# A two-block transformer on one core: latent and cross-attention queries computed turned, the first feed-forward steps reordered, the input loaded in quarters

## The reference

```python
# block 1
h = h + 0.5 * swiglu(rmsnorm(h, ffn1_norm), ffn1_w_gu, ffn1_w_down)   # hidden width 2816
# ... sparse and block attention of 8 heads each, gates, w_out ...
h = h + 0.5 * swiglu(rmsnorm(h, ffn2_norm), ffn2_w_gu, ffn2_w_down)
# block 2, layer 0 mixer: latent attention (8 heads, 128 + 64 rope dimensions)
lat = h @ w_dkv
c_q, c_kv, k_pe = rmsnorm(lat[:384], g_q), rmsnorm(lat[384:640], g_kv), lat[640:]
q, kv = c_q @ w_uq, c_kv @ w_ukv
# causal softmax over [q, rope(q_pe)] . [k, rope(k_pe)], then @ w_o
# layer 1 mixer: stick-breaking attention. After each mixer:
h = h + mem_cross_attn(rmsnorm(h), rmsnorm(mem), w_q, w_kv, w_o)      # 4 heads of 128, 256 memory rows
h = h + square(relu(rmsnorm(h) @ w_in)) @ w_out                       # hidden width 4096
```

## Time and profile before

| | |
|---|---|
| time, median of 3 runs | 1272.52 us (1272.42 to 1272.82) |
| profiled execution: time | 1272.93 us |
| profiled execution: span of its instructions | 1271.0 us |
| PE busy | 1257.9 us (99%) |
| PE weight loads busy | 1081.4 us |
| DVE busy | 756.7 us (60%) |
| ACT busy | 656.1 us (52%) |
| POOL busy | 21.1 us |

### The profile page before, as it was taken

How to read it: one execution, slowest core, us unless ns; L and a number is a source line. 1 busy time by engine, 2 the same in 40 slices (tenths; PEclk the granted TensorE clock), 3 DMA queues, 4 the chain that set the end, 5 groups by cost and what they waited for, 6 DMA issues and landing times.

```text
span 1271.0 us, 16754 instructions
## 1 busy us (share of the span) xinstructions
PE 1257.9 (99%) x6734; PEld 1081.4 (85%) x6734; DVE 756.7 (60%) x1056; ACT 656.1 (52%) x846; POOL 21.1 (2%) x25
## 2 busy tenths in 40 slices
PE   9999999999999999999999999999999999999997
PEld 7888888888888888889888799989888887999896
DVE  6555448788675554447765675454553655754553
ACT  6454437464455444436954564443465745643433
POOL 0000000001000000000000000000000000000001
PEclk9999999999999999999999999999999999999999
DMA  8855546554533655544633265554565332665540
GB/s 291 291 178 197 185 151 209 217 182 138 177 133 125 242 180 195 179 135 169 240 125 116 83 240 192 199 177 135 185 232 184 115 108 91 226 216 176 195 133 34
DMA packets 39213, 221.71 MB, mean 174 GB/s; under 512 B 4486, under 2 KB 5142, under 8 KB 23649
## 3 DMA queue, kind: packets, MB, share of 16 engines
q1 hardware_dynamic: 36672, 214.20, 48.8%
q0 software_dynamic: 1024, 4.22, 1.0%
q10 hardware_dynamic: 1440, 2.22, 0.6%
HBM read 219.56 MB, written 1.07 MB: 174 GB/s over the span
## 4 chain that ended last, share of the span: by engine, by line
PE 93%; DVE 3%; ACT 2%; issue 1%; DMA 1%; POOL 0%; SPq 0%; DVEq 0%; ACTq 0%
PE ps L403 23%; PE ps L405 23%; PE ps L404 23%; PE ps L612 5%; PE ps L611 5%; PE ps L610 5%; PE ps L1424 2%; PE ps L1449 2%; PE ps L437 1%; DVE wlo L368 1%; PE ps L984 1%; PE ps L1436 1%; PE ps L643 1%; DMA w_raw<-ffn_first 1%; ACT whi L360 0%
## 5 line engine op out<-in xcount | busy, mean ns | idle before, releaser
L368 DVE TENSOR_TENSOR wlo<-w_raw,whi 128x2048 fp32r<-128x2048 f32 (+4 forms) x244 | 468.5, 1927 | 379.2 <-ACT whi L360 379.0
L360 ACT ACTIVATE whi<-w_raw 128x2048 fp32r<-128x2048 f32 (+4 forms) x244 | 393.3, 1618 | 407.3 <-PE ps L405 304.9
L403 PE MATMUL ps<-whi,xt_h 128*128 128x512 f32 (+3 forms) x784 | 308.8, 394 | 1.5 <-DVE nat L790 0.8
L405 PE MATMUL ps<-whi,xt_l 128*128 128x512 f32 (+3 forms) x784 | 302.5, 386 | 0.0
L404 PE MATMUL ps<-wlo,xt_h 128*128 128x512 f32 (+3 forms) x784 | 301.8, 385 | 0.0
L403 PE MATMUL ps<-whi,ot_h 128*128 128x512 f32 x594 | 235.1, 396 | 0.0
L405 PE MATMUL ps<-whi,ot_l 128*128 128x512 f32 x594 | 231.7, 390 | 0.0
L404 PE MATMUL ps<-wlo,ot_h 128*128 128x512 f32 x594 | 231.4, 390 | 0.0
L403 PEld LDWEIGHTS ps<-whi,xt_h 128*128 128x128 f32 x784 | 147.3, 188 | 32.7 <-issue 4.8
L405 PEld LDWEIGHTS ps<-whi,xt_l 128*128 128x128 f32 x784 | 147.1, 188 | 29.6
L404 PEld LDWEIGHTS ps<-wlo,xt_h 128*128 128x128 f32 x784 | 147.4, 188 | 27.3
(11 more groups left out here) (227 smaller groups left out, 875.7 us busy)
## 6 DMA issues: line engine op xcount, KB each, us to landing
w_raw<-ffn_mid SPq DMA_DIRECT2D x80, 768.0 KB, 4.3
w_raw<-mlp_mid SPq DMA_DIRECT2D x56, 1024.0 KB, 5.0
w_raw<-w_qkv SPq DMA_DIRECT2D x12, 1024.0 KB, 5.0
w_raw<-w_sb_qkv SPq DMA_DIRECT2D x12, 1024.0 KB, 4.9
w_raw<-w_xkv SPq DMA_DIRECT2D x8, 1024.0 KB, 4.9
w_raw<-ffn_first SPq DMA_DIRECT2D x8, 512.0 KB, 4.4
w_raw<-w_gate_b SPq DMA_DIRECT2D x4, 1024.0 KB, 4.9
w_raw<-w_gate_a SPq DMA_DIRECT2D x4, 1024.0 KB, 5.0
```

Of the source, the lines that this page charges most:

```text
L360: nc.scalar.activation(whi[:, s, 0:tiles * width], w_raw[:, s, 0:tiles * width], ACT.Copy).then_inc(w_hi, 1)
L368: nc.vector.tensor_tensor(wlo[:, s, 0:tiles * width], w_raw[:, s, 0:tiles * width], whi[:, s, 0:tiles * width].bitcast(F32), ALU.subtract) ...
L403: nc.tensor.matmul(acc, hi, whi[:, s, c], start=start, stop=False)
L405: return nc.tensor.matmul(acc, lo, whi[:, s, c], start=False, stop=stop)
```

## The change

It has four parts.

1. **Latent queries and keys turned** (`LatentUp` in place of the `Project` named `mla_up`). The rope queries come first, in the usual form. The eight query heads and the eight key heads are made in the turned form, two heads (a pair) per bank. A token's row factor can no longer be applied per partition. For the queries it moves into the exponent's scale and the peak (`row`, `minus`); for the keys it is spread over partitions by two products (`diagonals` against ones) and multiplied in by DVE when it takes the keys out of the bank (`take_k`).
2. **Cross-attention queries turned**, head by head, row factor in the exponent; the fourth head's products stand between the scores; the groups are ordered by pair of heads; DVE scales all four; the projection's pieces are reordered.
3. **First step of the gated feed-forwards**: in ffn2 the last two chunks go by token tile (`second_half`); in ffn1 the products of a tile run as high parts first (`first_tensor`), and chunk 4's low part is split in two pieces around `nat` of tile 0 (`second_lo`).
4. **x in four quarters**, one between each two of the first weight chunks; chunks 0 to 2 are split tile by tile; three wake products instead of two behind the first transposes.

The core of the diff:

```diff
+            def tensor(self, pe):                                  # LatentUp
+                before = self.before
+                pe.wait_ge(before.lows, NT)
+                for t in range(NT):
+                    pe.wait_ge(before.evac, t + 1)
+                    self.rows(pe, self.pe, t, 0, 3)
+                before.turn(pe, before.units[-1])
+                for p in range(4):
+                    pe.wait_ge(self.evac, p + 1)
+                    self.pair(pe, self.q[p // 2], p, 0, 3)
+                self.aside.tensor(pe)
...
+                pe.wait_ge(self.diagonal, 1)
+                for t in range(NT):
+                    last = nc.tensor.matmul(bankT[0][:, t * P:(t + 1) * P], const[:, C_ONES:C_ONES + P],
+                                            self.diagonals[:, t * P:(t + 1) * P], start=True, stop=True)
+                last.then_inc(self.spread, 1)
+                for p in range(4):
+                    if p < 2:
+                        pe.wait_ge(self.evac, 5 + p)
+                    else:
+                        pe.wait_ge(self.k_taken, p - 1)
+                    self.pair(pe, self.k[p // 2], p, 3, 2)
+                self.turn(pe)
...
+            def scalar(self, act):
...
+                next_hi(act, self.q[1])
+                self.aside.scalar(act)
+                act.wait_ge(self.spread, 1)
+                nc.scalar.activation(self.factors, bankT[0][:, 0:S], ACT.Copy).then_inc(self.spread_in, 1)
+                next_hi(act, self.k[0])
+                self.take_turned(act)
+                act.wait_ge(self.before.rooted, 2)
+                self.take_v(act, 0)
+                next_hi(act, self.k[1])
+                self.take_v(act, 1)
+                next_hi(act, self.v[0])
+                next_hi(act, self.v[1])
...
+            def vector(self, dve):
+                self.factor(dve)
+                self.rotate(dve, 0)
+                self.rotate(dve, 1)
+                next_lo(dve, self.pe)
+                next_lo(dve, self.q[0])
+                next_lo(dve, self.q[1])
+                self.aside.vector(dve)
+                self.take_k(dve, 0)
+                self.take_k(dve, 1)
+                next_lo(dve, self.k[0])
+                self.take_k(dve, 2)
+                self.take_k(dve, 3)
+                next_lo(dve, self.k[1])
+                next_lo(dve, self.v[0])
+                next_lo(dve, self.v[1])
```

```diff
             def tensor(self, pe):                                  # CrossAttention
...
+                self.query(pe, [0, 1], [2, 3])
+                self.query(pe, [2], [0, 1, 2, 3])
+                take_chunk(pe, self.q0 + 1)
+                self.query(pe, [0, 1, 2], [4, 5])
+                self.query(pe, [0, 1, 2], [6, 7])
                 pe.wait_ge(*self.keys_ready)
+                pe.wait_ge(cross_taken, NXH * i + 2)
                 att.score(pe, 0)
                 att.score(pe, 1)
+                used(self.query(pe, [3], [0, 1, 2, 3]), self.q0)
+                self.query(pe, [3], [4, 5, 6, 7])
+                att.turn(pe, 0)
+                pe.wait_ge(cross_taken, NXH * (i + 1))
                 att.score(pe, 2)
                 att.score(pe, 3)
+                att.turn(pe, 1)
                 pe.wait_ge(*self.values_ready)
                 att.value(pe, 0)
+                att.value(pe, 1)
                 att.turn(pe, 2)
                 att.turn(pe, 3)
                 att.value(pe, 2)
                 att.value(pe, 3)
```

```diff
+                if self.name == "ffn1":                            # Ffn.vector, behind the root
+                    second_lo(dve, 0)
+                    self.hide_vector(dve, 0, (0,))
+                    second_lo(dve, 1)
+                    self.hide_vector(dve, 0, (1,))
                 else:
-                    next_lo(dve, self.n0)
-                self.hide_vector(dve, 0)
+                    if self.gated:
+                        next_lo(dve, self.n0)
+                    self.hide_vector(dve, 0)
...
+            for part in range(3):                                  # ACT's start; DVE's is alike
+                pair_scalar(act, "ffn1", part)
+                first_hi(act, part)
+            pair_scalar(act, "ffn1", 3)
             split_hi(act, 3)
...
-            wake(2)
-            norm_tensor(pe, "ffn1", 0, (1,))
+            wake(3)
```

More of the change, by code:

```diff
@@ L294, in build @@
         ident_in = sem("ident_in")
-        x_in = [sem(f"x_in{part}") for part in range(3)]
-        first_tile = sem("first_tile")
+        x_in = [sem(f"x_in{part}") for part in range(4)]
+        tile_hi = sem("tile_hi")
+        tile_lo = sem("tile_lo")
         blanks = sem("blanks")
@@ L2132, in gpsimd @@
                 pass
-        class CrossAttention:
-            def __init__(self, i, fills, q_unit, groups, fins, like=None):
-                self.cross, self.mlp = f"cross{i}", f"mlp{i}"
-                self.q = Project(f"mem_q{i}", f"xq{i}", [q_unit], xt_h, xt_l, norm=self.cross)
-                self.unit = q_unit
-                self.att = Attend(f"mem{i}", groups, fins, [], turned=True, bare=True, like=like and like.att)
-                self.fin, self.keys_ready, self.values_ready = self.att.fin, fills[0].ready, fills[1].ready
-                self.n0 = AT[f"xo{i}"]
-                self.full = sem(f"mem_out{i}_full")
-                ends[self.n0], ends[self.n0 + 1] = (self.full, NT), (self.full, NB * NT)
-            def query(self, pe, n, t, ks):
-                for k in ks:
-                    if t == 0 and k % 2 == 0:
-                        xt_ready(pe, self.cross, k)
-                    last = mm3(bankA[t], xt_h[:, k, t * P:(t + 1) * P], xt_l[:, k, t * P:(t + 1) * P],
-                               slot_of(n), k % 4, TW, k == 0, k == KC - 1)
-                if ks[-1] == KC - 1:
-                    last.then_inc(self.q.full, 1)
+        cross_q = sem("cross_q")
@@ new lines, in build, with __init__, q_bank, query @@
+        cross_taken = sem("cross_taken")
+        cross_out_hi = sem("cross_out_hi")
+        cross_out_lo = sem("cross_out_lo")
+        cross_full = sem("cross_full")
+        class CrossAttention:
+            def __init__(self, i, fills, groups, like=None):
+                self.i, self.cross, self.mlp = i, f"cross{i}", f"mlp{i}"
+                self.att = Attend(f"mem{i}", groups, [], [], turned=True, bare=True, like=like and like.att)
+                self.keys_ready, self.values_ready = fills[0].ready, fills[1].ready
+                self.q0, self.n0 = AT[f"xq{i}"], AT[f"xo{i}"]
+                self.full0 = NB * NT * i
+                ends[self.q0 + 1] = (cross_q, NXH * (i + 1))
+                ends[self.n0], ends[self.n0 + 1] = (cross_full, self.full0 + NT), (cross_full, self.full0 + NB * NT)
+            def q_bank(self, head):
+                return (bankA + bankT)[head][:, 0:S]
+            def query(self, pe, heads, ks):
+                for head in heads:
+                    for k in ks:
+                        if head == 0 and k % 2 == 0:
+                            xt_ready(pe, self.cross, k)
+                        cols = slice(k % 4 * TW + head * P, k % 4 * TW + (head + 1) * P)
+                        n = slot_of(self.q0 + k // 4)
+                        nc.tensor.matmul(self.q_bank(head), whi[:, n, cols], xt_h[:, k], start=k == 0, stop=False)
+                        nc.tensor.matmul(self.q_bank(head), wlo[:, n, cols], xt_h[:, k], start=False, stop=False)
+                        last = nc.tensor.matmul(self.q_bank(head), whi[:, n, cols], xt_l[:, k], start=False,
+                                                stop=k == KC - 1)
+                    if ks[-1] == KC - 1:
+                        last.then_inc(cross_q, 1)
@@ L2587, in mla_groups @@
                         group.append(dict(
-                            at=i * keys, width=keys, tile=t, head=hd,
+                            at=i * keys, width=keys, tile=t, head=hd, row=qrow(t), minus=mla_up.minus(0, t),
                             bias=const[:, C_CAUSAL + S - keys:C_CAUSAL + S],
```

442 lines of the change are left out of this document (291 added, 151 removed).

## The result

| | before | after |
|---|---|---|
| median of 17 runs | 1272.76 us (1272.34 to 1273.16) | 1274.70 us (1274.13 to 1275.87) |
| ratio to before | | 1.0017, 95% interval 1.0011 to 1.0024 |
| profiled span | 1271.0 us | 1272.6 us |

The forecast was 1273.6, 1269.6 to 1276.6, and the result lies inside the 0.2% that the prediction called no change. The sum came close, but two of its terms were too small, in opposite directions.

The account below looks back on a forecast made before the run. It took TensorE's own work (93% of the chain) and its few waits as the bound. Latent +3.4, cross-attentions -2.2, ffn2 0, start -0.2 gave +1.0: 1273.95 profiled, median 1273.6 us, range 1269.6 to 1276.6.

Parts of the forecast that it names:

- likeliest case: The exchange as summed over all stages, without any rival: 55%.
- Latent stage: Latent up-projection to first attention turn: 2.3 us less TensorE work, but waits on DVE; net +3.4, between +2.7 and +4.2.
- first pause: Latent stage, ahead of key pair 2: TensorE waits about 4.0 us for DVE's take_k(0).
- Pairs 2 and 3 (2.9 and 0.1 of restart): Latent stage: key pairs 2 and 3 behind TensorE's wait take 2.9 us plus 0.1 of restart, ending at 626.4.
- The clock rival: The granted clock falls in the latent stage's new pause, costing 2.9 us more: 1276.5; chance 10%.
- The second pause: At the first attention turn TensorE, there at 641.8, waits 2.3 us for a turn at 644.1.
- The start: ffn1's start with x in quarters and high parts first: -0.2 us, bounds -0.8 and +0.3.
- ACT's row sums then come 0.5 later: In ffn1's start ACT's extra half-width splits and four moved transposes delay its row sums, and DVE's root, by 0.5 us.
- start 7.8 to 8.2: TensorE's first real product in ffn1 comes at 7.8 to 8.2 us, against 8.43 before.
- Cross-attention: Both cross-attentions, turned queries and reordered work: -1.1 us each, -2.2 together; bounds -0.35 and -1.4 each.
- ffn2, 0: ffn2 by token tile gives nothing, since TensorE still waits for DVE's nat behind the same split.
- DVE not late: Latent stage: TensorE doesn't wait for DVE's key copy, so the stage gives -2.3 us: 1267.8; chance 15%.

Follow-up runs that it names:

- busy_pause: The changed kernel with six spare fp32 products on TensorE ahead of key pair 2 in the latent stage: 1274.29 us, ratio 1.0009 to the kernel before.
- keys_first: The changed kernel with DVE taking the keys ahead of the memory norm's low parts and row factors spread ahead of the memory transposes: 1270.47 us, ratio 0.9978.
- keys_busy: keys_first with four spare fp32 products on TensorE ahead of the first attention turn: 1268.97 us, ratio 0.9971 to the kernel before.
- start_only: The kernel before with only the change's start (x in quarters, splits by tile, high parts first, three wake products): 1271.87 us, ratio 0.9992.
- x_early: logits_first with the third and fourth quarter of x loaded together, ahead of chunk 2: 1267.37 us.
- ffn2_undone: logits_first without the call of second_half, so ffn2's last chunks run as before the change: 1266.91 us.
- logits_first: keys_first with DVE's last low part of the latent stage moved behind the first two groups' logits and the first scaling: 1266.89 us, ratio 0.9955.
- const_scale: The changed kernel with a constant exponent scale and 1.0 on the peaks, leaving out the queries' row factor: 1274.04 us, ratio 1.0013.

## Why the prediction came out as it did

The time was in the range and within 1.1 us of the forecast, but it was not the likeliest case that happened as described. The prediction had named a dip of the granted clock in this stretch as a sign of being wrong, and the dip came.

- **Latent stage, +3.4 forecast, +5.1 in the profile, 4.7 in the medians.** The mechanism was right to a tenth as far as the first pause: `take_k(0)` was to free PE 22.67 behind the stage's start, and it did at 22.70. Behind it the term was too small twice. "Pairs 2 and 3 (2.9 and 0.1 of restart)" took 4.47, since the clock fell: 1.5 of the 1.7 missing. The exponents were priced at 0.40; with a scale read from memory they take 0.49, 0.4 over the four on the path. The later steps (values, the last two splits, the logits) kept their distances, each 1.3 to 1.4 late.
- **The clock rival** had 10% and a price of 2.9. It happened, on top of the forecast: 1.5 in the profile of the change and 1.2 of its time by busy_pause, 1.5 between keys_first and keys_busy. I had priced all 24 key products at half rate, 0.24 each; the first 17 took 0.21, and 3.6 us behind PE's restart the rate was back up. What spoke against it in my text, that pauses of 1.23 leave the clock up, was no evidence about 3.75. The Trainium skill (TensorE: Matmul & The Clock Gate, section "Why this matters for your kernels") says that such a gap sends the clock back to half; the 0.57 at 622 agrees, and I should have put this case into the forecast.
- **The second pause**, 2.3 forecast, 2.43 measured. What I didn't see is that it, too, can drop the clock. It did in the profiles of busy_pause (2.43) and keys_first (2.25), and not in that of the change, where the clock had fallen 20 us earlier. The change's upper group, seven of 17 times and 1.3 above the lower, is the size of such a second fall, and keys_busy, with that pause covered, has no upper group.
- **The start, -0.2 forecast with a bound of -0.8; -1.25 in the profile and -1.0 in time, outside that bound.** The step that failed is "ACT's row sums then come 0.5 later". They came earlier, 15.04 in start_only and 14.70 in the change, for 15.37 before. I had added the fixed cost of two splits and left out that ACT stood 1.87 us at 12.03 waiting for chunk 2, whose load stood behind half of x. In the changed kernel ACT's only wait for a load there is 0.30, at the first chunk. x_early puts the loads at 0.5, not clear of the spread. And "start 7.8 to 8.2" was late: PE starts at 7.22 and 7.59. What keeps it going then are the high parts first: with the transposes between the products, waiting for the low parts costs 2.0.
- **Cross-attention, -1.1 each; -1.18 and -1.12 in the profile.** Point by point: 0.83 less up to the projection (forecast 0.75), 0.35 in it (forecast 0.3). In the profile all four waits on POOL, 3.0 us in both stages, are gone and 1.0 of waits on DVE has come. Alone on the kernel before they gave the same in the profile, 1.6 in the median, and 2.2 is inside its interval.
- **ffn2, 0**: so in the profile and in ffn2_undone.
- **DVE not late** (the faster rival): false as forecast, but it is what the change could have been. With two changes of order (keys_first and logits_first) the same instructions take 1266.89.

By the profiles the two misses, +1.7 and -1.05, nearly cancelled: +1.6 instead of +1.0. That the time came so close is luck. The last step of the sum was rounded up besides: 1272.52 + 1.0 is 1273.5, not 1273.6.

## What to carry to other kernels

When an edit moves a copy out of PSUM to another engine, count what stands ahead of it in that engine's queue, and place it ahead of work that nobody waits for soon; here two changes of order decided between 0.17% slower and 0.45% faster. A long pause of TensorE can have two prices, its own length and the slow products behind it (here behind pauses of 3.75, 2.43 and 2.25), and with the first pause covered the next one can still bring the second price. Where the times of a kernel stand in groups, compare group with group: here the medians hid two thirds of what covering the first pause gave. At the start of a kernel, read for each engine which load it waits for before adding up fixed costs.

## What the runs showed of the hardware that I had not expected

- The granted clock fell to the 1.2 GHz level behind pauses of 3.75, 2.43 and 2.25 us, and not behind others of 2.43 (the changed kernel) and 1.99 (const_scale). In the times of the changed kernel, busy_pause, keys_first and const_scale both outcomes seem to stand side by side, 1.0 to 1.5 apart. The profiles fit: clock up behind the second pause in the lower groups (the changed kernel, const_scale), down in the upper ones (busy_pause, keys_first). No kernel has a profile of both.
- The rate of PE's first products rises at different moments in executions of nearly the same code: the four transposes ahead of the first split took 0.62 in the changed kernel and 1.06 in start_only.
- ScalarE's exponent of 128x128 takes 0.49 with a scale per partition from memory and 0.40 with a constant; of 128x256, 0.60 and 0.51.
